# Sliding attention in a two-block transformer kernel: probabilities divided on GpSimd, output pairs made turned in two column strips

## The reference, cut to what matters

```python
q = partial_rope_2(q_in.reshape(B, S, 16, 64), positions)
k = partial_rope_2(k_in.reshape(B, S, 2, 64), positions)
v = v_in.reshape(B, S, 2, 64)
# per block of 128 queries, keys of the block before and of its own
s = q @ k^T * 64 ** -0.5, masked to 0 <= distance < 128
m = max(max_k(s), sink)
p = exp(s - m)
out = (p @ v) / (sum_k(p) + exp(sink - m))
merged = sigmoid(ga) * (dn_out @ w_up_dn) + sigmoid(gb) * (out @ w_up_sw)
x = x + rmsnorm(merged @ w_o, post_mix_g)   # then an MLP, likewise
```

## Time and profile before

| | us |
|---|---|
| median of 3 executions (1834.23 to 1835.99) | 1834.26 |
| the profiled execution | 1833.58 |
| its span, first to last instruction | 1831.8 |
| TensorE busy | 1774.7 |
| VectorE busy | 1146.7 |
| ScalarE busy | 908.2 |
| GpSimd busy | 212.4 |

### The profile page before, as it was taken

How to read it: one execution, slowest core, us unless ns; L and a number is a source line. 1 busy time by engine, 2 the same in 40 slices (tenths; PEclk the granted TensorE clock), 3 DMA queues, 4 the chain that set the end, 5 groups by cost and what they waited for, 6 DMA issues and landing times.

```text
span 1831.8 us, 27947 instructions
## 1 busy us (share of the span) xinstructions
PE 1774.7 (97%) x10679; PEld 1454.0 (79%) x10679; DVE 1146.7 (63%) x2135; ACT 908.2 (50%) x1640; POOL 212.4 (12%) x354
## 2 busy tenths in 40 slices
PE   5999999999999999999999999999999999999998
PEld 4878878888788788777787778887878787778887
DVE  5656667665656677586655665556687655675554
ACT  4345376443545645575344354445575434455443
POOL 0300200021030000301112000000311211100000
PEclk9999999999999999999999999999999999999999
DMA  7543544555444455533222455554532222455552
GB/s 244 175 161 118 176 131 153 183 186 188 133 139 160 139 181 173 166 115 115 70 72 92 145 178 200 188 186 128 197 118 91 92 93 70 141 161 182 184 186 90
DMA packets 136971, 270.07 MB, mean 147 GB/s; under 512 B 5516, under 2 KB 8584, under 8 KB 136840
## 3 DMA queue, kind: packets, MB, share of 16 engines
q1 hardware_dynamic: 134964, 265.52, 43.6%
q10 hardware_dynamic: 1876, 2.78, 0.5%
HBM read 267.23 MB, written 1.05 MB: 146 GB/s over the span
## 4 chain that ended last, share of the span: by engine, by line
PE 86%; DVE 6%; ACT 3%; issue 2%; POOL 2%; DMA 1%; SPq 0%; DVEq 0%; POOLq 0%; ACTq 0%
PE bank L381 23%; PE bank L383 23%; PE bank L382 22%; PE bank L405 4%; DVE buf L1876 1%; PE bank L1544 1%; PE bank L1560 1%; PE bank L1451 1%; PE bank L1563 1%; POOL scratch L914 1%; PE bank L562 1%; DMA raw<-in_w_in 1%; DVE buf L1874 1%; PE bank L1515 1%; DVE lo L363 0%
## 5 line engine op out<-in xcount | busy, mean ns | idle before, releaser
L381 PE MATMUL bank<-hi,xh 128*128 128x512 f32 (+1 forms) x2016 | 819.2, 406 | 10.8 <-DVE xl L452 6.9
L383 PE MATMUL bank<-hi,xl 128*128 128x512 f32 (+1 forms) x2016 | 788.7, 391 | 0.0
L382 PE MATMUL bank<-lo,xh 128*128 128x512 f32 (+1 forms) x2016 | 786.1, 390 | 0.0
L363 DVE TENSOR_TENSOR lo<-raw,hi 128x1024 fp32r<-128x1024 f32 (+1 forms) x504 | 605.7, 1220 | 52.4 <-PE bank L383 40.4
L353 ACT ACTIVATE hi<-raw 128x1024 fp32r<-128x1024 f32 (+1 forms) x504 | 520.4, 1049 | 221.7 <-PE bank L383 217.0
L381 PEld LDWEIGHTS bank<-hi,xh 128*128 128x128 f32 x2016 | 381.0, 189 | 91.9 <-issue 13.6
L383 PEld LDWEIGHTS bank<-hi,xl 128*128 128x128 f32 x2016 | 380.1, 189 | 82.6
L382 PEld LDWEIGHTS bank<-lo,xh 128*128 128x128 f32 x2016 | 381.9, 189 | 68.6
L405 PE MATMUL bank<-square,buf 128*128 128x128 f32 x584 | 88.0, 273 | 3.4 <-POOL buf L919 1.4
L405 PEld LDWEIGHTS bank<-square,buf 128*128 128x128 f32 x584 | 70.0, 140 | 20.7 <-issue 4.8
L1773 ACT ACTIVATE scratch<-bank 128x256 f32<-128x256 f32 (+1 forms) x48 | 18.3, 382 | 122.7 <-PE bank L1544 106.0
(11 more groups left out here) (285 smaller groups left out, 1720.0 us busy)
## 6 DMA issues: line engine op xcount, KB each, us to landing
raw<-in_w_in SPq DMA_DIRECT2D x136, 1024.0 KB, 5.1
raw<-in_w_ff SPq DMA_DIRECT2D x64, 1024.0 KB, 5.4
raw<-in_w_proj_a SPq DMA_DIRECT2D x8, 1024.0 KB, 5.0
raw<-in_w_proj_b SPq DMA_DIRECT2D x8, 1024.0 KB, 5.0
raw<-in_w_out SPq DMA_DIRECT2D x8, 1024.0 KB, 5.1
raw<-in_w_up_sw SPq DMA_DIRECT2D x8, 1024.0 KB, 5.0
raw<-in_w_up_dn SPq DMA_DIRECT2D x8, 1024.0 KB, 5.0
raw<-in_w_o SPq DMA_DIRECT2D x8, 1024.0 KB, 5.0
```

What stands on the lines that cost most here:

```text
L363: dve.tensor_tensor(self.lo[g % LO_RING][:, 0:w], src, self.hi[g % HI_RING][:, 0:w].bitcast(F32), ALU.subtract).then_inc(self.lo_ready, 1)
L381: pe.matmul(out, xh[:, row, t], self.hi[slot % HI_RING][:, w], start=first, stop=False)
L382: pe.matmul(out, xh[:, row, t], self.lo[slot % LO_RING][:, w], start=False, stop=False)
L383: mm = pe.matmul(out, xl[:, row, t], self.hi[slot % HI_RING][:, w], start=False, stop=last)
```

## The change

The plan's `work` now comes from `sliding`: in slot t stand, in this order, the outputs of heads t - 4 and t - 3 together (even t from 4), the turn of t - 2, the division (`s_scale`) of t - 1 and the scores of t. It has one slot more, t = 18, the second slot of `gb`, where the last pair's outputs stand ahead of `betas`.

- GpSimd multiplies the probabilities of a head (128 and 256 columns) by the reciprocal, once VectorE has made it; the turn waits for that. `prob` has three buffers instead of two, `turned` two instead of one.
- The outputs of two heads are made with v as the stationary operand, 64 columns wide, and the turned probabilities as the moving one: the result has the head dimension on the partitions, head t - 4 on 0 to 63 and head t - 3 on 64 to 127 of the bank `OUT`, 256 tokens wide. Four matmuls per pair.
- ScalarE copies that to `xh[1]`, VectorE subtracts it for `xl[1]`. The product with the reciprocal into `ys`, the four turns of `ys` and their cuts are gone.

```diff
--- before.py
+++ after.py
@@ -204,6 +204,18 @@
                    + ([(f"{kind}_turn", t - 1)] if 1 <= t <= heads else [])
...
     return out
+
+
+def sliding(heads):
+
+    slots = []
+    for t in range(heads + 3):
+        scores = [("s_scores", t)] if t < heads else []
+        scale = [("s_scale", t - 1)] if 1 <= t <= heads else []
+        turn = [("s_turn", t - 2)] if 2 <= t <= heads + 1 else []
+        out = [("s_out", t - 3)] if t >= 4 and t % 2 == 0 else []
+        slots.append(out + turn + scale + scores)
+    return slots
 
...
 def difference(heads):
@@ -1031,7 +1043,7 @@
     p.run([Job("ba0", "w_in_2", 0, at_sw, KB, small, 4, 0, 0, SCORE)])
...
 
-    work = [w[:1] + w[:0:-1] if len(w) == 3 else w for w in attention("s", HEADS)]
+    work = sliding(HEADS)
     p.run(sec("dk", D), [[("rope", "sk", 0), ("rope", "sk", 1), ("rope", "sq", 0)], [("rope", "sq", 1)], [], [],
...
     conv = lambda n: [[("turn", n, (0, 2, 4, 6).index(i))] if i in (0, 2, 4, 6) else [] for i in range(8)]
@@ -1040,7 +1052,7 @@
     p.run(sec("dv", 2 * D), [a + b + c for a, b, c in zip(work[9:17], conv("dq"), norms)])
...
     slots = [[] for _ in range(64)]
-    for at, steps in ((0, work[17] + [("rows", 0)]), (1, [("betas", 0), ("turn", "dv", 0)]),
+    for at, steps in ((0, work[17] + [("rows", 0)]), (1, work[18] + [("betas", 0), ("turn", "dv", 0)]),
                       (2, [("silu", "dq")]), (3, [("gram", 0), ("square", "dq")]),
...
         slots[at] += steps
@@ -1091,9 +1103,7 @@
     rest = {(0, "y1"): [("turn", "dv", 1)], (0, "t1"): [("squares", "dq")], (0, "y2"): [("turn", "dv", 2)], (0, "y3"): [("turn", "dv", 3)], (0, "y5"): [("silu", "dv")],
...
             (1, "t3"): [("turn", "v", 1)], (1, "t4"): [("turn", "v", 2)], (1, "y6"): [("turn", "v", 3)],
-            (1, "t6"): [("turn", "kd", 1)],
-            (2, "t3"): [("turn", "ys", 0)], (2, "t4"): [("turn", "ys", 1)], (2, "y6"): [("turn", "ys", 2)],
-            (2, "t6"): [("turn", "ys", 3)]}
+            (1, "t6"): [("turn", "kd", 1)]}
     out = []
...
         before = finish(g - 1) if g else {}
@@ -1108,7 +1118,6 @@
               "delta_u": OUT, "delta_s": TURN, "delta_r": OUT, "delta_v": TURN, "delta_o": OUT}
...
              ("v", 0): OUT, ("v", 1): OUT, ("v", 2): OUT, ("v", 3): OUT, ("kd", 0): TURN, ("kd", 1): TURN,
-             ("ys", 0): OUT, ("ys", 1): OUT, ("ys", 2): OUT, ("ys", 3): TURN,
              ("dk", 0): 2, ("dk", 1): 3, ("dk", 2): 0, ("dk", 3): 1,
...
 
@@ -1251,16 +1260,16 @@
     ks = flat8[:, 512:1024].rearrange("p (k t) -> p k t", t=S)
...
     k_dec = flat8[:, 0:1024].rearrange("p (h d) -> p h d", d=P)
-    source = {"sq": b0, "sk": k_dup, "dq": b0, "dk": b1, "dv": b1, "ys": ys, "yd": vb,
+    source = {"sq": b0, "sk": k_dup, "dq": b0, "dk": b1, "dv": b1, "yd": vb,
               "mix": qs}
-    xt_of = {"ys": 1, "yd": 0, "mix": 1}
-    half_of = {"ys": 1.0, "mix": 0.5}
+    xt_of = {"yd": 0, "mix": 1}
+    half_of = {"mix": 0.5}
     tap = lambda j, n: 2 * KB + 1 + j * 3 * DHEADS + n
...
     scr = core.scratch
-    prob = [scr[:, i * 384:(i + 1) * 384] for i in range(2)]
+    prob = [scr[:, first:first + 384] for first in (0, 384, 2688)]
     masked = [scr[:, 768 + i * 384:768 + (i + 1) * 384] for i in range(2)]
-    turned = scr[:, 2304:2688]
+    turned = [scr[:, first:first + 384] for first in (1536, 2304)]
     junk = scr[:, 3072:4096]
...
     def region(first, n, *shape):
@@ -1341,7 +1350,7 @@
                         for b in job.banks:
...
                     if n == 0:
-                        ready = {"us0": ("cut", ("ys", 3))}.get(job.name)
+                        ready = {"us0": ("cut", ("ys", HEADS - 1))}.get(job.name)
                         if ready:
...
                         if job.name[:2] == "dn":
@@ -1405,7 +1414,7 @@
                     core.free(pe, b)
...
                             "dq": ("conv_in", "dq1"), "dk": ("conv_in", "dk1"), "dv": ("conv_in", "dv1"),
-                            "ys": ("ys", HEADS - 1), "yd": ("yd_gated", f), "mix": ("mix", f // 2),
+                            "yd": ("yd_gated", f), "mix": ("mix", f // 2),
                             "v": ("silu", "dv"), "kd": ("silu", "dk")}.get(arg) or ("evac", f"up{arg[1:]}")
...
                     if arg == "v":
@@ -1469,21 +1478,23 @@
                 if kind == "s_turn":
...
                     core.free(pe, TURN)
-                    pe.wait_ge(*at("s_prob", h))
+                    pe.wait_ge(*at("s_scaled", h))
                     for c in range(3):
-                        mm = pe.transpose(B[TURN][:, c * P:c * P + P], prob[h % 2][:, c * P:c * P + P], core.ident)
+                        mm = pe.transpose(B[TURN][:, c * P:c * P + P], prob[h % 3][:, c * P:c * P + P], core.ident)
                     mm.then_inc(*up("s_turned", h))
...
                 if kind == "s_out":
+
                     h = arg
...
                     v = slice(HD * (h // (HEADS // 2)), HD * (h // (HEADS // 2)) + HD)
-                    pe.matmul(B[OUT][:, 0:HD], turned[:, 0:P], vs[:, 0, v], start=True, stop=True)
-                    pe.matmul(B[OUT][:, HD:2 * HD], turned[:, P:2 * P], vs[:, 0, v], start=True, stop=False)
-                    pe.matmul(B[OUT][:, HD:2 * HD], turned[:, 2 * P:3 * P], vs[:, 1, v],
-                              start=False, stop=True).then_inc(*up("s_summed", h))
-                    core.hold(s, OUT, "ys", h)
+                    for i, r in enumerate(halves):
+                        pe.matmul(B[OUT][r, 0:S], vs[:, 0, v], turned[i][:, 0:S], start=True, stop=False)
+                    for i, r in enumerate(halves):
+                        mm = pe.matmul(B[OUT][r, P:S], vs[:, 1, v], turned[i][:, S:S + P], start=False, stop=True)
+                    mm.then_inc(*up("s_summed", h))
+                    core.hold(s, OUT, "cut", ("ys", h))
                 b = delta_bank(kind, arg) if kind in DELTA_BANK else None
...
 
@@ -1736,10 +1747,10 @@
                 if kind == "s_scores":
...
                     act.wait_ge(*at("s_max", h))
-                    if h >= 2:
-                        act.wait_ge(*at("s_turned", h - 2))
+                    if h >= 3:
+                        act.wait_ge(*at("s_turned", h - 3))
                     for tb, cols, _ in parts:
-                        act.activation(prob[h % 2][:, cols], masked[h % 2][:, cols], ACT.Exp, scale=-1.0,
+                        act.activation(prob[h % 3][:, cols], masked[h % 2][:, cols], ACT.Exp, scale=-1.0,
                                        bias=t1.negmax[:, h % 2, tb:tb + 1],
...
                     act.wait_ge(*at("s_sink", h))
@@ -1747,9 +1758,12 @@
                 if kind == "s_turn":
...
                     act.wait_ge(*at("s_turned", h))
-                    if h >= 1:
-                        act.wait_ge(*at("s_summed", h - 1))
-                    act.activation(turned, B[TURN][:, 0:3 * P], ACT.Copy).then_inc(*up("s_copied", h))
+                    if h >= 2:
+                        act.wait_ge(*at("s_summed", h - 1 - h % 2))
+                    act.activation(turned[h % 2], B[TURN][:, 0:3 * P], ACT.Copy).then_inc(*up("s_copied", h))
+                if kind == "s_out":
+                    act.wait_ge(*at("s_summed", arg))
+                    act.activation(core.xh[1][:, arg // 2, :], B[OUT][:, 0:S], ACT.Copy).then_inc(*up("high", ("ys", arg)))
                 if kind == "rows":
...
                     act.activation(score[arg % 2], decay[arg % 2], ACT.Exp).then_inc(*up("decay_exp", arg))
@@ -1997,17 +2011,14 @@
                     negative_max(dve, core, s, B[SCORE[h % 2]], masked[h % 2], t1.negmax[:, h % 2, :], parts, 2,
...
                                  t.negsink_all[:, layer, h:h + 1])
-                if kind == "s_turn":
+                if kind == "s_scale":
                     h = arg
...
                 if kind == "s_out":
-                    h = arg
-                    dve.wait_ge(*at("s_summed", h))
-                    dve.wait_ge(*at("s_inverse", h))
-                    dve.tensor_tensor(ys[:, :, h * HD:h * HD + HD],
-                                      B[OUT][:, 0:2 * HD].rearrange("p (t d) -> p t d", t=TB),
-                                      bcast(t1.inverse[:, h % 4, :], 2, HD), ALU.mult).then_inc(*up("ys", h))
+                    dve.wait_ge(*at("high", ("ys", arg)))
+                    dve.tensor_tensor(core.xl[1][:, arg // 2, :], B[OUT][:, 0:S], core.xh[1][:, arg // 2, :].bitcast(F32),
+                                      ALU.subtract).then_inc(*up("cut", ("ys", arg)))
                 if kind == "rows":
...
                     dve.wait_ge(*at("rows", arg))
@@ -2123,11 +2134,16 @@
                     pool.wait_ge(*at("s_max", h))
...
                                        ALU.subtract).then_inc(*up("s_sink", h))
-                if kind == "s_turn":
+                if kind == "s_scale":
                     h = arg
...
```

(5 more changed lines are left out.)

## The result

The kernel after the change took 1852.74 us (median of 4, 1849.97 to 1855.04) against 1835.12 us before (median of 4): ratio 1.0093 [1.0072, 1.0114]. The forecast was 1837.6 us with a range up to 1843.0. The direction was right, and the size five times too small: +17.6 us instead of +3.3. The profiled execution took 1855.04 us (span 1853.2, mean granted clock 0.988; before, span 1831.8 and 0.993); it is the slowest of the four, two of which took 1850.0 and 1850.6 at a clock of 0.990.

What follows compares the result with a forecast made beforehand. TensorE was busy 97% of the span, but VectorE would eat its gain in the plain slots. +4.35 at `betas` less 2.7 gave +1.65 a layer, +3.3 us for two: 1836.9, as median 1837.6 us, range 1831.5 to 1843.

Steps and rivals of the forecast that it cites:

- Pair of outputs, 0.84 us: Attention, TensorE: column strips side by side take 0.64 us, with two shape changes at 0.1 each 0.84, for 1.22 before.
- Rival C: Attention outputs on TensorE: column strips go one after the other, 1.3 to 1.9 us more a layer; chance 0.13.
- Turns of `ys`, -2.7 us a layer: Delta rule: dropping four turns and VectorE's cuts gains 1.8 + 0.7 + 0.2 = 2.7 us a layer.
- GpSimd's multiply at 1.0 us: Attention: GpSimd's multiply of 128 and 256 columns takes 1.0 us a head for both parts.
- Rival B: GpSimd's multiply is slower than its neighbours: each 0.5 us costs 2.5 a layer, 1842.6 us; chance 0.18.
- The collision, "the split waits 0.45": Attention, each pair: VectorE's split of the weights waits 0.45 us because GpSimd's multiply is still running.
- A pair at 8.9 us on VectorE: Plain attention slots: VectorE needs 8.9 us per pair of heads, against 8.93 before, eating TensorE's gain.
- Rows +2.5: Hand-over: head 15's late multiply and turn free the bank late; `rows` starts at 850.15 instead of 847.64, +2.5 us.
- Betas +1.9, 4.2 us behind rows: Hand-over: `betas` waits behind the last outputs, copy and cut, 4.2 us after `rows` instead of 2.34, +1.9 us.
- The clock, "none did in the old 1.47": New waits: a falling clock would make all slower; none fell in the old 1.47 us wait; no size given.

Runs made afterwards that it cites:

- run 4: The kernel before, with only the four turns of `ys` in the delta rule and their cuts left out: 1828.6 us, ratio 0.9973.
- run 6: The change, but GpSimd multiplies only 56 of 128 and 112 of 256 columns: 1841.4 us, ratio 1.0033 against the kernel before.
- run 2: The narrow kernel: the change, but GpSimd's two multiplications of a head cover 2 columns each: 1832.4 us, ratio 0.9997 against the kernel before.
- run 13: The kernel before, with its last output moved behind rows and betas: 1830.4 us, ratio 0.9974.

## Why the prediction was wrong, by its own steps

- **Pair of outputs, 0.84 us.** Right (0.80). Rival C, strips one after the other, did not happen.
- **Turns of `ys`, -2.7 us a layer.** Right: 5.5 us in run 4 for two layers, and -2.96 (11.52 to 8.56) and -2.58 (24.09 to 21.51) in the table.
- **GpSimd's multiply at 1.0 us: the step that failed.** It measured 1.51. I placed it by the two-input rows, 0.46 and 0.74 each, and set its lower bound from a record of two columns; the range of 0.6 to 1.1 did not hold it. Rival B had the mechanism and priced 0.5 us at 2.5 a layer, 5 us in all; from 0.96 us (run 6) to 1.51 (the change) it cost 1.0033 to 1.0093, 11 us, and 12.6 at equal clock. What B and the sum did not have is the loop: all of a long multiply goes through GpSimd's queue into VectorE's reciprocal, in every pair, and through the hand-over's waits into rows and betas.
- **The collision, "the split waits 0.45".** The wrong way round. The multiply is two instructions, and VectorE's split slipped between them: it kept its 1.22 us and the multiply became 2.49. VectorE did not become the bound by its own work; its reciprocal waited 1.61 where I had 0.8. The Trainium skill, SBUF — State Buffer, Who interferes with whom, calls the shared ports an exclusive lock, held by a VectorE instruction with two SBUF inputs against a GpSimd one that reads SBUF. The trace agrees to about 0.15 us: the second part, at 784.46, was 1.90 us long in place of 0.92, and the split had 1.12 us to go.
- **A pair at 8.9 us on VectorE.** 9.36, and for another reason, the loop through GpSimd's queue; at the forecast's duration it is 8.59 (run 6). The attention up to its last slots was to cost nothing in all and cost 3.0.
- **Rows +2.5.** From slot 15 to rows +3.06, with the wait for the turn at 2.84 where I had about 2.
- **Betas +1.9, 4.2 us behind rows.** The mechanism was right to 0.1 us where the clock stays up: 4.29 in run 2 (845.36 to 849.65). In the change it is 5.84, since the half piece and the outputs run at the lower clock. A further +1.9 comes from slow stretches up to 884.
- **The clock, "none did in the old 1.47".** I named it as what would make all slower and gave it no price. It is the second term, and it was put at nothing: behind waits of 2.84, 0.58 and 0.94 us in a row it fell, and over all executions it cost about 4 of the 17.6 us. That the old clock stayed up behind the 1.47 is true of the windows up to 820, but it fell twice a layer in the old trace too, at 825 to 835 and 870 to 880. First layer in sum: +3.0 slots, +3.1 rows, +3.5 betas, +1.9 behind them, -3.0 turns = +8.5, where the forecast was +1.65. The second layer, with a clock sum of 12.0 us, lost 13.0 (8.56 to 21.51).

The 4.5 us by which the second layer loses more have two sources. 1.05 lie ahead of its attention, where TensorE waits for GpSimd's rotary step (TensorE, before and after):

```profile
1316.78 0.63 PE L405 MATMUL bank<-square,buf 128*128 128x128 f32 x4 [0.19 <-POOL buf L919]
```

```profile
1326.40 0.63 PE L417 MATMUL bank<-square,buf 128*128 128x128 f32 x4 [1.24 <-POOL buf L931]
```

The change has no part in it: the narrow kernel has 0.17 there, and the kernel before has 1.24 at the same place of its first layer. The other 3.4 are the clock's: it loses 6.9 us more than before in the second layer (12.0 for 5.1) and 3.5 more in the first (10.3 for 6.8).

What stays open: why the granted clock falls for longer in one layer or execution than in another with the same instructions. And no run set the clock while it kept the waits; its price of 0.9 is read from the scatter of executions.

## What to carry to other kernels

Work moved to a slow in-order engine is priced by what is queued behind it: here a subtraction of 0.29 us stood behind the multiply, and with that subtraction elsewhere two thirds of the loss was gone, the multiply as slow as before. Where TensorE crosses from one stage to the next, start the long dependent chain first and the tail of the old stage behind it; this alone was worth as much as the whole loss. When two kernels differ by less than one scatters, look at the granted clock of every execution before you believe the difference, as run 13 shows. And bound an operation that no row shows generously from above: a missed duration passes through the queue, then the wait, then the clock.
